# Decode attention loads each page of cache A onto 64 partitions, two rows to a partition

## The reference, cut to what matters

```python
past = (cache_a_kv[l][page_table].reshape(db, past_len, 2, H_A, HEAD), ...)
...
kv_a = new_a if past is None else jnp.concatenate([past[0].astype(new_a.dtype), new_a], axis=1)
oa = diff_attention(qa, kv_a[:, :, 0].reshape(B, L, H_A, 2, DQ_A), kv_a[:, :, 1], q_pos, jnp.arange(L), lam)
...
def diff_attention(q, k, v, q_pos, k_pos, lam):
    s = jnp.einsum('bqhcd,bkhcd->bchqk', qb.astype(jnp.float32), kf) * scale
    p = masked_softmax(s, k_pos[None, :] <= pos[:, None])
    w = p[:, 0] - lam * p[:, 1]
    return jnp.einsum('bhqk,bkhv->bqhv', w, vf)
```

## Time and profile before

| | us |
|---|---|
| median of 3 runs | 2168.87 (2167.9 to 2170.78) |
| the profiled execution | 2162.88 |
| its span in the profile | 2160.8 |
| decode attention, from its first page load to its last weighted sum | 1312.6 to 1802 |
| share of the DMA engines' time in use, 1310 to 1790 | 0.98 |
| busy share of PE over the whole span | 81% |

### The profile page before, as it was taken

How to read it: one execution, slowest core, us unless ns; L and a number is a source line. 1 busy time by engine, 2 the same in 40 slices (tenths; PEclk the granted TensorE clock), 3 DMA queues, 4 the chain that set the end, 5 groups by cost and what they waited for, 6 DMA issues and landing times. The chain is left out here.

```text
span 2160.8 us, 38449 instructions
## 1 busy us (share of the span) xinstructions
PE 1748.9 (81%) x14577; PEld 1350.7 (63%) x14577; DVE 856.0 (40%) x1568; ACT 584.7 (27%) x1233; POOL 116.0 (5%) x143
## 2 busy tenths in 40 slices
PE   6999989999866888979729966788878884119999
PEld 5888878887655555766627754666656662117777
DVE  4222212222274323134166633455555554692221
ACT  4211211221122111111143312454445442441110
POOL 3000000000000000000040010000000000440000
PEclk9999999999988877899958957999999997559999
DMA  6555655533422111242460007999999992432442
GB/s 195 177 183 180 198 151 182 185 118 100 133 71 78 46 54 54 88 106 63 145 246 25 25 14 282 367 359 363 363 352 364 362 365 72 189 107 75 132 129 72
DMA packets 214312, 365.74 MB, mean 169 GB/s; under 512 B 41837, under 2 KB 121390, under 8 KB 211734
## 3 DMA queue, kind: packets, MB, share of 16 engines
q1 hardware_dynamic: 213414, 360.64, 49.1%
q10 hardware_dynamic: 288, 2.10, 0.2%
q0 software_dynamic: 432, 0.63, 0.2%
HBM read 328.54 MB, written 39.02 MB: 170 GB/s over the span
## 5 line engine op out<-in xcount | busy, mean ns | idle before, releaser
L316 PE MATMUL pj_ps<-pj_whi,pj_xhi 128*128 128x512 f32 (+1 forms) x1024 | 419.7, 410 | 7.1 <-PEq L83 4.3
L317 PE MATMUL pj_ps<-pj_wlo,pj_xhi 128*128 128x512 f32 (+1 forms) x1024 | 404.1, 395 | 0.0
L318 PE MATMUL pj_ps<-pj_whi,pj_xlo 128*128 128x512 f32 (+1 forms) x1024 | 403.0, 394 | 0.0
L249 DVE TENSOR_TENSOR pj_wlo<-pj_w,pj_whi 128x1024 fp32r<-128x1024 f32 (+1 forms) x128 | 153.2, 1197 | 535.7 <-ACT pj_whi L221 533.5
L221 ACT ACTIVATE pj_whi<-pj_w 128x1024 fp32r<-128x1024 f32 (+1 forms) x128 | 132.6, 1036 | 585.0 <-DMA pj_w<-in_w_in 583.1
L316 PEld LDWEIGHTS pj_ps<-pj_whi,pj_xhi 128*128 128x128 f32 x1024 | 199.6, 195 | 67.4 <-issue 28.8
L318 PEld LDWEIGHTS pj_ps<-pj_whi,pj_xlo 128*128 128x128 f32 x1024 | 199.2, 195 | 40.9
L317 PEld LDWEIGHTS pj_ps<-pj_wlo,pj_xhi 128*128 128x128 f32 x1024 | 200.0, 195 | 34.2
L1299 PE MATMUL da_tp<-all_ident,da_pa 128*128 128x128 f32 x1024 | 149.6, 292 | 48.6 <-DMA da_pb<-in_cache_b_kv 47.1
L1419 ACT ACTIVATE da_kT<-da_tp 128x512 f32<-128x512 f32 x200 | 119.2, 596 | 224.5 <-PE da_tp L1299 224.5
L1299 PEld LDWEIGHTS da_tp<-all_ident,da_pa 128*128 128x128 f32 x1024 | 119.5, 148 | 69.7 <-DMA da_pb<-in_cache_b_kv 57.5
(11 more groups left out here) (507 smaller groups left out, 2441.5 us busy)
## 6 DMA issues: line engine op xcount, KB each, us to landing
da_pa<-in_cache_a_kv SPq DMA_DIRECT2D x256, 512.0 KB, 5.5
pj_w<-in_w_in SPq DMA_DIRECT2D x120, 512.0 KB, 4.7
px_pages<-in_cache_b_kv SPq DMA_DIRECT2D x256, 128.0 KB, 2.4
da_pb<-in_cache_b_kv SPq DMA_DIRECT2D x256, 128.0 KB, 6.0
ou_w<-in_w_out SPq DMA_DIRECT2D x32, 512.0 KB, 3.8
proj<-pj_out SPq DMA_DIRECT2D x60, 256.0 KB, 5.6
ap_rows_p<-proj SPq DMA_DIRECT2D x4, 1408.0 KB, 15.0
da_pw<-in_state_b_win SPq DMA_DIRECT2D x8, 512.0 KB, 7.7
```

The source lines that it names most:

```text
L249: dve.tensor_tensor(self.wlo[:, r, :, 0:n], self.w[:, r, :, 0:n], self.whi[:, r, :, 0:n], ALU.subtract).then_inc(self.wlo_ready, 1)
L316: pe.matmul(acc, hi, high, start=kc == 0, stop=False)
L317: pe.matmul(acc, hi, low, start=False, stop=False)
L318: last = pe.matmul(acc, lo, high, start=False, stop=kc == KC - 1)
```

## The change

Only the load of a page of cache A is altered. Page i of a group of four now fills 64 partitions: pages 0 and 2 the partitions 0 to 63, pages 1 and 3 the partitions 64 to 127. Partition p of such a half holds rows 2p and 2p+1 of the page side by side, 2048 floats. Pages 0 and 1 lie in the blocks 0 and 1 of the ring place, pages 2 and 3 in the blocks 2 and 3. Block c therefore holds the odd or even rows of two pages, where it held one page.

```diff
@@ decode_attend, block.sync
                         for i in range(4):
-                            sp.dma_start(pa[:, m % RING, i, :], d.cache_a[bass.ds(pages[i], 1), :, :]
-                                         .rearrange("a p n -> p (a n)")).then_inc(loaded[m % RING], 16)
+                            half = slice(64 * (i % 2), 64 * (i % 2) + 64)
+                            sp.dma_start(pa[half, m % RING, 2 * (i // 2):2 * (i // 2) + 2, :], d.cache_a[bass.ds(pages[i], 1), :, :]
+                                         .rearrange("a (p x) n -> p (a x) n", x=2)).then_inc(loaded[m % RING], 16)
                             sp.dma_start(pb[:, m % RING, i, :], d.cache_b[bass.ds(pages[i], 1), :, 256:512]
                                          .rearrange("a p n -> p (a n)")).then_inc(loaded[m % RING], 16)
```

## The result

The changed kernel takes 2492.7 us in the median of four runs (2479.23 to 2504.96), the kernel before 2168.39 us in as many. The ratio is 1.149, with a 95% interval of 1.143 to 1.156. It is slower by some 324 us. That is inside the stated range of 2340 to 2500 us by 7 us, 58 us above the point forecast, and above the 2420 to 2480 us that the forecast gave its main case.

What follows compares the result with a forecast made beforehand. The DMA engines, slightly ahead of PE, were taken to bound decode attention. Page A at 616 us plus an unchanged 121 made 737 us per engine, 270 above 467: 2433 us, stated as 2435, range 2340 to 2500 us.

Steps and rivals of the forecast that it cites:

- main case: Decode attention: engines sharing ways into SBUF stay in step; kernel at 2420 to 2480 us, chance 0.50.
- rival D: Decode attention: lower PE clock, waits that don't overlap, or loads at 187 GB/s give 2480 to 2560 us; chance 0.07.
- The bound: Decode attention: DMA engines in front at 467 us against PE's 434; slower loads cost one for one almost at once.
- Term 1: Page A loads: half as many, longer packets save fixed cost, 11 us gained, other bound 28.
- Term 2: Page A loads onto 64 partitions: 602 ns a packet, 616 us per engine; stage 270 us more than 467.
- the two ends: Page A packets onto 64 partitions: 327 ns (no harm) or 602 ns (same harm as 32 partitions); 602 taken.
- all the rest 121 us: Decode attention: engine time for all but page A's packets, B's loads included, taken as unchanged at 121 us.
- Term 3: Alternating halves in flight together in decode attention: engines stay in step, so nothing added.
- rival A: Decode attention: sharing engines partly out of step, +201 us, 2370 us as a median; chance 0.27.
- Rival B: Decode attention: 64-partition loads run at full rate, packets under some 340 ns, 2140 to 2158 us; chance 0.12.
- Rival C: Page A loads: packets stay 4096 bytes or HBM holds today's rate, no difference, 2165 to 2173 us; chance 0.04.
- What was to show it: Decode attention: DMA share 0.95 or more, about 230 GB/s, some 750 us; PE's load wait about 300 us.

Runs made afterwards that it cites:

- The two kernels on 128 partitions: Changed kernel with one DMA loading two neighbouring pool pages onto all partitions: 2148 us with 8192-byte packets, 2151 us with 4096-byte packets.
- Page A alone: Changed kernel without group B's page loads after the first four groups: 2330 us, ratio 1.075.
- quarters: Changed kernel with each page on 32 partitions, four rows to a partition, packets of 16384 bytes: 2515 us.
- every second partition: Changed kernel with each page on the even or the odd partitions instead of a block of 64: 2186 us, ratio 1.009.
- with one queue and with two: Changed kernel with pages 0 and 2 from SP's queue, 1 and 3 from ACT's, in place of SP's alone: 2500 us, ratio 1.153.

## Why the prediction was right, point by point

The direction, the stage and the main term were right for the stated reasons. The size was met with little to spare: the main case ended at 2480 us and the measured 2493 us lie in the band of rival D, 2480 to 2560 us, of which the range took in the lowest 20. That the range held is in part luck.

**The bound.** Right. A stage at a DMA share of 0.98 gave a slower load back one for one, and nothing hid it.

**Term 1, the fixed cost of a packet.** 11 us forecast, with 28 as the other bound. The two kernels on 128 partitions show 11 us by their packet times. The Trainium skill's 3 cycles a packet ("DMA: Bandwidth & Descriptors", "Why small descriptors are slow (HBM only)") would have been an estimated 3.5 ns; the packet times show about 11.

**Term 2, the reach of a load.** Right in mechanism and size. 602 ns was read off the 32-partition loads, with the 34 short packets of that window counted in; the 67 packets' own records have 593 in the mean. Page A alone took 593 in a long stream by the share, 586 by the records. By the packet records page A's part of an engine grew from 352 to 623 us, 271, where the forecast had 270. What the runs show is that the set of partitions decides; that engines meet in twos on ways that they share is inferred from the rate, which halves, and was not seen engine by engine. The choice between the two ends, which the rows did not settle, was right: quarters and halves cost the same, within 1%. The Trainium skill ("SBUF — State Buffer", "Door 1: The DMA port swizzle (why `[64,N]` ≈ `[32,N]`)") says that partitions 0 to 63 reach the same 8 ports as 0 to 31, for some 218 GB/s in a long transfer; page A alone, whose loads alternate between the halves, ran 2% above that, at 223 GB/s. By that section of the Trainium skill, the ports follow from bits of the partition number of which the lowest is not one, so that even partitions reach all 16. The 344 GB/s of every second partition agree with that too.

**The term that was mis-sized** is the one that I carried over unchanged, "all the rest 121 us". It holds B's loads, which still write 128 partitions and whose packets did not change. Between page loads of 64 partitions they cost 0.68 us instead of 0.41, 65 us in all. Page A alone, 9 to 17 us cheaper than the forecast's 616, takes some of that back; 48 to 56 us are left, and the result has 54 above the 270. The packet records agree: the 1024-byte packets grew by 79 us, page A by 271 and the short packets by 6; the 32 us beyond 324 are records that overlap and time in which the engines had been idle. I had priced the rest by its own packets, as if its neighbours on the engines did not matter, when the point of the whole term was that they do.

**Term 3 and rival A.** No relief came from alternating halves, as the sum had it, and rival A's 2370 us did not happen. The reason given for no relief, that engines which share stay in step, is not borne out, since the order of the halves moves the time by 1%; the sum was right there without its reason. But rival A is not right for that: the free stretches that it counted on are missing: of the 8192-byte packets in the changed kernel from 1400 to 1780 us, 0.3% took under 350 ns, though the times spread widely (a tenth under 485, a tenth over 694). Nor do the engines win at page A what they lose at B: page A's packets are longer in the mix (609 ns) than alone (586).

**Rival B** fell, with one queue and with two; its point of decision, packets under 340 ns, was met only with all 128 partitions (322 ns), and nearly with every second one (350 ns). **Rival C** fell by the packet counts. **Rival D** had two halves. The half of the clock cost nothing: the granted clock did fall, from 0.95 to 0.80 in the stage, and the transposes of page A took 379 ns in the mean where they took 292, but PE's busy time rose only from 384 to 470 us and stayed far below the transfers' 802. The other half, slower loads "in a mix of shapes", is what happened, only smaller and elsewhere: page A's packets ran at 215 GB/s (8192 × 16 bytes in 609 ns) and not at 187, and it was B's loads that slowed most. The forecast had the right case at a chance of 0.07 and left it out of the sum.

**What was to show it.** 45151 packets under 8 KB (forecast some 45 thousand), PE's wait 295 us (about 300), the stages around within 2 us, all right. The 216 GB/s in place of 230, and the stage of some 802 us in place of 750, are B's loads again.

## What to carry to other kernels

Longer packets are worth little once they are 4096 bytes (11 ns for each one saved here), while the set of partitions that one DMA writes can halve its rate; ask that first of any new layout. If a layout needs only 64 partitions, take every second one rather than a block: 2186 against 2493 us, with one slice changed. And when a term of a sum slows the engines down, price again what shares them, though it is itself unchanged.

## What the runs showed of the hardware beyond that

The 128-partition loads of 128 KB, placed between loads onto a block of 64, took 0.68 us where their packets alone make 0.41: a 1024-byte packet took 82 ns in place of 47.5. Collecting them four in a row recovered only 9 to 16 of the 65 us, and that at the page loads; B's packets stayed at 80 ns. In the kernel before, the same collecting gave 0.3%. Between loads onto every second partition B's packets were not slowed (46.9 ns).
